# Seven sums of squares moved half a block or a whole block later in TensorE's order

## The chip, the cores and the metric

The program runs on one core of a Trainium2 chip. The metric is the device time of one execution in microseconds (us), and lower is better. PE is TensorE, DVE is VectorE, ACT is ScalarE, POOL is GpSimd, SP is the engine that issues the weight transfers.

## The reference

Two transformer blocks run one after the other on 256 tokens of width 1024. All projections are dense matrix products with a normed activation; there are five feed-forward layers (one with a convolution, four with SwiGLU), a recurrence with its own attention, a gated chunk mixer, and two cross-attentions onto a memory of 256 rows. What matters here is the norm in front of a projection:

```python
def rms_norm(x, g):
    x32 = x.astype(jnp.float32)
    y = x32 * lax.rsqrt(jnp.mean(x32 * x32, axis=-1, keepdims=True) + RMS_EPS)
    return (y * g.astype(jnp.float32)).astype(x.dtype)

def swiglu_ffn(h, w_in, w_out):
    gate, up = jnp.split(h @ w_in, 2, axis=-1)
    return (jax.nn.silu(gate) * up) @ w_out

# per layer
x = x + 0.5 * swiglu_ffn(rms_norm(x, ffn1_norm[i]), ffn1_w_in[i], ffn1_w_out[i])
...
x = x + memory_cross_attention_2(rms_norm(x, xattn_norm[i]), mem_k, mem_v, xattn_wq[i], xattn_wo[i])
x = x + 0.5 * swiglu_ffn(rms_norm(x, ffn2_norm[i]), ffn2_w_in[i], ffn2_w_out[i])
```

## The kernel before

**The stream of weights.** The activations lie feature by feature over the 128 partitions, 8 tiles of 256 tokens. All weights come as 288 blocks of 1 MB in one fixed order. SP loads a block into one of two buffers `raw` as soon as DVE has finished with the block two before. A block has two halves ("pieces") of 1024 columns. ACT copies a piece to `wh`, rounded to the matmul's format (function `high`, L1267), DVE takes the difference `raw - wh` into `wl` (function `low`, L1890), and PE multiplies with three products per tile pair (`split_mm`, L282): 24 matmuls of 128x256 for a piece, 48 for a block. There are four slots of `wh` and `wl`, so the copies of block b+2 (issued by `high(b)` and `low(b)`) wait until PE is done with the same half of block b (semaphore `piece_done`).

**Late norms.** Seven of the norms are "late": `ffn0`, `ffn1`, `x0`, `ffn2`, `ffn3`, `x1` and `ffn4` (five feed-forward layers and two cross-attentions, in this order in time: ffn0, ffn1, x0, ffn2, ffn3, x1, ffn4). There the product runs with the activation that has only its gain, and the factor `rstd` is multiplied into the result, so PE need not wait for it. Meanwhile ACT squares x in two halves, DVE sums each half over its 4 tiles (`norm_parts`, L1919, one reduction for each half, into `work`), and PE sums over the partitions with a matrix of ones (`norm_sum`, L371, one fp32 matmul for each half; the page counts each as two). ACT then makes `rstd` from the sum with a Ln (L1299) and an Exp (L1306), each behind an `ACT_TABLE_LOAD`.

**Orders around a late norm.** Each engine runs its own list in the order written. PE in a feed-forward layer: first block, `norm_sum`, second block, four small matmuls that clear the accumulators (L409, behind a wait for `norm_var`, which the Ln sets), then steps of two blocks of the up projection and one of the down projection. In `ffn1` the sum of another norm (`mem2`) and a third sum (`first_norm_sum`, 16 rows at L379) stand at the same place. PE in a cross-attention: query block 0, `norm_sum`, query blocks 1 and 2, scores of head 0 (L920, which wait until DVE has scaled query block 0 with `rstd`), query block 3, and so on. DVE stands in front of every such place with the `low` of the second block, then the reduction of the second half of the squares, then the `low` of the third block, then the wait for `rstd`. ACT: `late_norm`, `high` of the third block, Ln, Exp, then in a feed-forward layer `early` (a Silu or the convolution's middle tap), `high` of the fourth block, `late`; in a cross-attention the `high` of the fourth block and of the next segment's first.

Of the kernel before, what the change touches and what calls it, by code (L numbers as in the profile page):

```python
# [51 lines left out]
BANKS = 4  # L52
# [222 lines left out]
def tensor_program(pe, t, s):  # L275
# [46 lines left out]
                              start=hf == 0 and tb == 0 and kk == 0, stop=k == KT - 1, weights_move=True)  # L322
        mm.then_inc(s["piece_done"], 1)

    def up_block(n, bank, b, act, name=None):
        for hf in range(2):
            up_piece(n, bank, b, hf, act, name)

    def token_block(n, bank, b, act, name=None):
# [55 lines left out]
    def ffn(f, seg, name):  # L385
# [10 lines left out]
                mm.then_inc(s["piece_done"], 1)  # L396

        up_block(n, n % BANKS, b, norm_parts, name)
        if f == 1:
            norm_sum("mem2")  # L400
        norm_sum(name)
        if f == 1:
            first_norm_sum(name)
        up_block(n + 1, (n + 1) % BANKS, b + 1, norm_parts)
        pe.wait_ge(s["norm_var"], NORM[name] + 1)
        if f == 0:
            pe.wait_ge(s["zero_row"], 1)
# [201 lines left out]
    for hf in range(2):  # L609
        w = piece(b, hf)  # L610
        for kk in range(4):
            k = 4 * hf + kk
# [333 lines left out]

    def memory_attention(i, name):
        project(f"xq{i}", norm_parts, n=1, name=name)
        norm_sum(name)
        project(f"xq{i}", norm_parts, first=1, n=2)  # L950
        scores, turn, mix = memory_heads(i)
        scores(0)
        project(f"xq{i}", norm_parts, first=3, n=1)
        scores(1)
        scores(2)
        turn(0)
        scores(3)
        for h in range(1, XA_H):
            turn(h)
            mix(h - 1)  # L960
        mix(XA_H - 1)
        for k in range(4):
            n = SEG[f"xo{i}"] + k
            bank_free(n)
            for hf in range(2):
                w = piece(BLK[f"xo{i}"] + k, hf)
                for kk in range(4):
                    c = 4 * hf + kk
                    if k == 0 and c % 2 == 0:
                        pe.wait_ge(s["att_low"], NA_H + CA_H + XA_H * i + c // 2 + 1)  # L970
                    for j in range(2):
                        mm = split_mm(ps[:, n % BANKS, j * T:(j + 1) * T],
                                      [x[:, kk * 256 + j * P:kk * 256 + (j + 1) * P] for x in w],
                                      [t.page_r[q][:, c * T:(c + 1) * T] for q in (2, 1)],
                                      start=c == 0 and j == 0, stop=c == KT - 1)
                mm.then_inc(s["piece_done"], 1)
# [275 lines left out]
def scalar_program(act, a, t, s):  # L1252
# [17 lines left out]
    def highs(seg, first=0, n=4):  # L1270
        for k in range(n):
            high(BLK[seg] + first + k)
# [297 lines left out]
    def ffn(fi, seg, early, late, prev=None, end=lambda *step: None):  # L1570
# [7 lines left out]
        if fi == 1:  # L1578
            joint_root(seg)
        else:  # L1580
            norm_root(seg)
        early(0, 0, 0, True)
        high(b + 1)
        late(0, 0, 0, True)
        end(0, 0, 0, True)

# [240 lines left out]

    def memory_attention(i, prev=None):
        late_norm(f"x{i}", prev)
        highs(f"xq{i}", n=1)  # L1830
        norm_root(f"x{i}")
        highs(f"xq{i}", 1, 2)
        memory_heads(i)
        highs(f"xo{i}", n=3)

# [39 lines left out]
def vector_program(dve, t, s):  # L1875
# [715 lines left out]

    def memory_attention(i, then, prev=None):
        late_norm(f"x{i}", prev)
        lows(f"xq{i}", n=1)
        dve.wait_ge(s["norm_std"], NORM[f"x{i}"] + 1)

        def query(k):
            if k:
                low(BLK[f"xq{i}"] + k)
            dve.wait_ge(s["piece_done"], 2 * (BLK[f"xq{i}"] + k) + 2)  # L2600
            scaled(t.page[0][:, k * 512:(k + 1) * 512],
                   ps[:, (SEG[f"xq{i}"] + k) % BANKS, :].rearrange("p (n t) -> p n t", n=2),
                   2).then_inc(s["u_evac"], 1)

        for k in range(3):
            query(k)
        memory_heads(i, query)
        residual(f"xo{i}", then=then)
# [238 lines left out]
```

## Time and profile before

| | us |
|---|---|
| three runs | 2081.5, 2084.69, 2081.97 |
| median | 2081.97 |
| the profiled execution | 2084.6 |
| its span | 2082.5 |
| PE busy | 1941.3 (93%) |
| DVE busy | 1331.4 (64%) |
| ACT busy | 1054.2 (51%) |
| mean granted clock | 0.978 |

The span is the time between the first and the last instruction in the trace; 2.1 us of the execution lie around it. A timeline row gives the start, the duration, the engine, the line, the operation and its operands, a count, and in brackets how long the engine sat idle before it and who ended that. The three runs differ by 3.2 us.

### The profile page before, as it was taken

How to read it: one execution, taken by the hardware profiler on the slowest of the kernel's cores; microseconds unless marked ns; L12 is line 12 of the kernel's file. 1: busy time of each engine (PE TensorE's matmuls, PEld its weight loads, DVE VectorE, ACT ScalarE, POOL GpSimd, SP SyncE). 2: the span in 40 equal slices, each digit the busy share in tenths (PEclk: the TensorE clock that was granted, in tenths of full speed). 3: DMA queues.
4: the chain of work that ended last, by engine and by line, in shares of the span. 5: the costliest groups of instructions: out<-in, count | busy, mean ns of one | idle time of the engine just before them, and what ended most of it. 6: DMA issues, size and time to landing. Idle time of an engine off the chain costs nothing.

```text
span 2082.5 us, 43630 instructions
## 1 busy us (share of the span) xinstructions
PE 1941.3 (93%) x18364; PEld 1894.7 (91%) x18364; DVE 1331.4 (64%) x1652; ACT 1054.2 (51%) x1373; POOL 56.9 (3%) x44
## 2 busy tenths in 40 slices
PE   5989997799998999998989899999999798999998
PEld 5988997799998999988888899999999797999998
DVE  6486579577777755698454656557555646556555
ACT  6555565745555544567522645445444455445443
POOL 0020000000000000000051000000000000000000
PEclk9999999899999999999999999999999899999999
DMA  5743332154554455443400335554445353434453
GB/s 196 223 152 140 132 132 102 61 183 162 184 186 149 166 181 181 169 155 120 164 5 3 144 120 182 181 181 163 181 181 183 124 183 116 160 124 166 183 183 113
DMA packets 51880, 313.35 MB, mean 150 GB/s; under 512 B 13488, under 2 KB 13616, under 8 KB 14256
## 3 DMA queue, kind: packets, MB, share of 16 engines
q1 hardware_dynamic: 51328, 308.42, 41.6%
q10 hardware_dynamic: 432, 3.15, 0.4%
q8 instruction: 97, 1.59, 0.3%
q14 instruction: 23, 0.19, 0.0%
HBM read 310.50 MB, written 1.05 MB: 150 GB/s over the span
## 4 chain that ended last, share of the span: by engine, by line
PE 68%; DVE 19%; ACT 6%; issue 4%; DMA 2%; DVEq 0%; ACTq 0%; SPq 0%
PE ps L282 60%; DVE wl L1890 6%; ACT wh L1267 2%; DMA raw<-in_stream 2%; PE ps L766 2%; DVE pages L2327 1%; DVE work L1919 1%; DVE pages L2147 1%; DVE pages L2149 1%; PE ps L941 1%; DVE pages L1963 1%; DVE pages L2389 1%; DVE h L1928 1%; DVE pages L2183 1%; DVE h_r L1948 1%
## 5 line engine op out<-in xcount | busy, mean ns | idle before, releaser
L1890 DVE TENSOR_TENSOR wl<-raw,wh 128x1024 fp32r<-128x1024 f32 x576 | 700.0, 1231 | 540.1 <-ACT wh L1267 538.4
L1267 ACT ACTIVATE wh<-raw 128x1024 fp32r<-128x1024 f32 x576 | 597.2, 1052 | 466.2 <-PE ps L282 403.5
L282 PE MATMUL ps<-sq_r,wh 128*128 128x256 f32 x2592 | 743.1, 287 | 17.9 <-DVE h_r L1907 8.3
L282 PE MATMUL ps<-sq_r,wl 128*128 128x256 f32 x2592 | 735.9, 284 | 0.0
L282 PE MATMUL ps<-h_r,wh 128*128 128x256 f32 x2560 | 727.1, 284 | 0.0
L282 PE MATMUL ps<-pages_r,wh 128*128 128x256 f32 x2480 | 550.4, 288 | 39.3 <-DVE pages_r L1907 18.4
L282 PEld LDWEIGHTS ps<-sq_r,wh 128*128 128x128 f32 x2592 | 500.2, 193 | 22.9 <-issue 18.9
L282 PEld LDWEIGHTS ps<-sq_r,wl 128*128 128x128 f32 x2592 | 500.1, 193 | 0.0
L282 PEld LDWEIGHTS ps<-h_r,wh 128*128 128x128 f32 x2560 | 494.2, 193 | 0.5
L282 PE MATMUL ps<-pages_r,wl 128*128 128x256 f32 x1680 | 480.6, 286 | 0.0
L282 PEld LDWEIGHTS ps<-pages_r,wh 128*128 128x128 f32 x2480 | 427.8, 196 | 43.5 <-issue 32.2
L282 PEld LDWEIGHTS ps<-pages_r,wl 128*128 128x128 f32 x1680 | 327.9, 195 | 0.0
L282 PE MATMUL ps<-work_r,wh 128*128 128x256 f32 x976 | 272.3, 286 | 0.0
L282 PEld LDWEIGHTS ps<-work_r,wh 128*128 128x128 f32 x976 | 187.3, 195 | 0.1
L1568 ACT ACTIVATE pages_r<-work 128x512 fp32r<-128x512 f32 x55 | 34.7, 632 | 152.2 <-DVE work L2362 124.2
L1645 ACT ACTIVATE work<-work 128x512 f32<-128x512 f32 x44 | 27.8, 632 | 76.6 <-DVE work L1963 76.5
L282 PE MATMUL ps<-wh,sq_r 128*128 128x256 f32 x224 | 64.1, 286 | 0.0
L282 PE MATMUL ps<-wh,h_r 128*128 128x256 f32 x224 | 63.4, 283 | 0.0
L282 PE MATMUL ps<-wl,sq_r 128*128 128x256 f32 x224 | 63.4, 283 | 0.0
L2246 DVE TENSOR_TENSOR work_r<-work,pages_r 128x512 fp32r<-128x512 f32 x55 | 38.1, 693 | 38.4 <-ACT pages_r L1568 38.4
L1624 ACT ACTIVATE pages<-pages,param 128x256 f32<-128x256 f32 x44 | 24.1, 595 | 49.0 <-DVE pages L1963 49.0
L1279 ACT ACTIVATE pages_r<-pages 128x512 fp32r<-128x512 f32 x48 | 29.8, 630 | 37.0 <-DVE pages L2389 23.0
(309 smaller groups left out, 1814.3 us busy)
## 6 DMA issues: line engine op xcount, KB each, us to landing
raw<-in_stream SPq DMA_DIRECT2D x288, 1024.0 KB, 4.8
pages<-in_rpb SPq DMA_DIRECT2D x32, 64.0 KB, 6.7
pages<-in_mem SPq DMA_DIRECT2D x1, 1024.0 KB, 5.3
x<-in_x SPq DMA_DIRECT2D x1, 1024.0 KB, 12.8
pages<-in_mem ACTq DMA_DIRECT2D x1, 1024.0 KB, 4.9
pages<-in_gmlp_b ACTq DMA_DIRECT2D x1, 1024.0 KB, 4.5
pages<-in_gmlp_w ACTq DMA_DIRECT2D x1, 1024.0 KB, 6.7
out<-h SPq DMA_DIRECT2D x4, 256.0 KB, 2.4
```

The source lines that it names most:

```text
L282: mm = pe.matmul(out, left, right, start=start and q == 0, stop=stop and q == 2, skip_group_check=True)
L766: mm = pe.matmul(ps[rows[par], bank + e, turned * 256 + u * CH:turned * 256 + (u + 1) * CH], left, right, start=True, stop=True)
L941: mm = pe.matmul(ps[:, memory_bank(i, "out", h), c * T:(c + 1) * T], t.page[15][:, at_:at_ + P], memory_turned(t, h)[:, mb * T:(mb + 1) * ...
L1267: f(t.wh[(2 * b0 + hf) % PIECE_SLOTS][:], t.raw[b0 % 2][:, hf * 1024:(hf + 1) * 1024], ACT.Copy).then_inc(s["high_done"], 1)
L1279: f(dst[:, c], src[:, c], ACT.Copy).then_inc(s["op_high"], 1)
L1568: f(hidden_parts(t, k)[0], t.work[:, k * 512:(k + 1) * 512], ACT.Copy).then_inc(s["hidden_high"], 1)
L1624: ins = f(t.page[k][:, j * T:(j + 1) * T], t.page[13][:, k * 1024 + j * T:k * 1024 + (j + 1) * T], ACT.Identity, scale=w, bias=bias)
L1645: f(gate_, gate_, ACT.Silu).then_inc(s["gate_ready"], 1)
L1890: tt(t.wl[i][:], t.raw[b0 % 2][:, hf * 1024:(hf + 1) * 1024], t.wh[i][:].bitcast(F32), ALU.subtract).then_inc(s["low_done"], 1)
L1919: dve.tensor_reduce(norm_partial(t, name)[:, hf * T:(hf + 1) * T], squares[:, hf * 1024:(hf + 1) * 1024].rearrange("p (k t) -> p t k", k=4 ...
L1928: stt(dst[:, c], src[:, c], par(t, gain[0], gain[1] + k), t.rstd[:] if rstd is None else rstd, ALU.mult, ALU.mult).then_inc(s["norm_out"], 1)
L2246: tt(low_, t.work[:, k * 512:(k + 1) * 512], high_.bitcast(F32), ALU.subtract).then_inc(s["hidden_ready"], 1)
```

## The change

The sum of squares leaves its place behind the first block. In the five feed-forward layers it stands behind the first half of the second block, with the other sums of `ffn1`; `up_block` gets a callback for that. In the two cross-attentions it stands behind query block 1, a whole block later. On ACT the `high` of the fourth block goes ahead of `early` in the feed-forward layers, and ahead of Ln and Exp in the cross-attentions; DVE's `low` of that block goes ahead of the wait for `rstd` in the cross-attentions. No instruction is added or removed.

```diff
--- before.py
+++ after.py
@@ -322,8 +322,10 @@
                               start=hf == 0 and tb == 0 and kk == 0, stop=k == KT - 1, weights_move=True)
         mm.then_inc(s["piece_done"], 1)
 
-    def up_block(n, bank, b, act, name=None):
+    def up_block(n, bank, b, act, name=None, between=lambda: None):
         for hf in range(2):
+            if hf:
+                between()
             up_piece(n, bank, b, hf, act, name)
 
     def token_block(n, bank, b, act, name=None):
@@ -396,12 +398,15 @@
                 mm.then_inc(s["piece_done"], 1)
 
         up_block(n, n % BANKS, b, norm_parts, name)
-        if f == 1:
-            norm_sum("mem2")
-        norm_sum(name)
-        if f == 1:
-            first_norm_sum(name)
-        up_block(n + 1, (n + 1) % BANKS, b + 1, norm_parts)
+
+        def sums():
+            if f == 1:
+                norm_sum("mem2")
+            norm_sum(name)
+            if f == 1:
+                first_norm_sum(name)
+
+        up_block(n + 1, (n + 1) % BANKS, b + 1, norm_parts, between=sums)
         pe.wait_ge(s["norm_var"], NORM[name] + 1)
         if f == 0:
             pe.wait_ge(s["zero_row"], 1)
@@ -946,8 +951,9 @@
 
     def memory_attention(i, name):
         project(f"xq{i}", norm_parts, n=1, name=name)
+        project(f"xq{i}", norm_parts, first=1, n=1)
         norm_sum(name)
-        project(f"xq{i}", norm_parts, first=1, n=2)
+        project(f"xq{i}", norm_parts, first=2, n=1)
         scores, turn, mix = memory_heads(i)
         scores(0)
         project(f"xq{i}", norm_parts, first=3, n=1)
@@ -1579,8 +1585,8 @@
             joint_root(seg)
         else:
             norm_root(seg)
+        high(b + 1)
         early(0, 0, 0, True)
-        high(b + 1)
         late(0, 0, 0, True)
         end(0, 0, 0, True)
 
@@ -1827,9 +1833,9 @@
 
     def memory_attention(i, prev=None):
         late_norm(f"x{i}", prev)
-        highs(f"xq{i}", n=1)
+        highs(f"xq{i}", n=2)
         norm_root(f"x{i}")
-        highs(f"xq{i}", 1, 2)
+        highs(f"xq{i}", 2, 1)
         memory_heads(i)
         highs(f"xo{i}", n=3)
 
@@ -2591,11 +2597,11 @@
 
     def memory_attention(i, then, prev=None):
         late_norm(f"x{i}", prev)
-        lows(f"xq{i}", n=1)
+        lows(f"xq{i}", n=2)
         dve.wait_ge(s["norm_std"], NORM[f"x{i}"] + 1)
 
         def query(k):
-            if k:
+            if k > 1:
                 low(BLK[f"xq{i}"] + k)
             dve.wait_ge(s["piece_done"], 2 * (BLK[f"xq{i}"] + k) + 2)
             scaled(t.page[0][:, k * 512:(k + 1) * 512],
```

The first place is PE at the start of `ffn2`; `sq_r` and `h_r` are the two parts of the activation, `wh` and `wl` those of the weights, and `low_done` is set by DVE's difference. Before:

```order
L282 MATMUL ps<-sq_r_50,wh 128x256
L282 MATMUL ps<-h_r_49,wh 128x256
L282 MATMUL ps<-sq_r_50,wl 128x256
L371 MATMUL ps<-work,const 128x256 [waits norm_part] x2
L282 MATMUL ps<-sq_r_50,wh 128x256 [waits low_done,u_evac]
L282 MATMUL ps<-h_r_49,wh 128x256
L282 MATMUL ps<-sq_r_50,wl 128x256
```

And the same place of the changed kernel, where a block's start is the row that waits for `u_evac` too, and a second half's start waits for `low_done` alone:

```order
L282 MATMUL ps<-sq_r_50,wh 128x256
L282 MATMUL ps<-h_r_49,wh 128x256
L282 MATMUL ps<-sq_r_50,wl 128x256
L373 MATMUL ps<-work,const 128x256 [waits norm_part] x2
L282 MATMUL ps<-sq_r_50,wh 128x256 [waits low_done]
L282 MATMUL ps<-h_r_49,wh 128x256
L282 MATMUL ps<-sq_r_50,wl 128x256
```

The sum stood in front of the second block and stands now in front of that block's second half, 24 matmuls later.

The second place is ACT in the cross-attention `x0`. `wh2`, `wh3` are the slots of the third block at first; `wh0`, `wh1` then take the fourth. Before:

```order
L1267 ACTIVATE wh2<-raw1 128x1024 [waits piece_done,raw_in1]
L1267 ACTIVATE wh3<-raw1 128x1024 [waits piece_done]
L1299 ACT_TABLE_LOAD
L1299 ACTIVATE rstd<-ps,stat 128x256 [waits norm_sum]
L1306 ACT_TABLE_LOAD
L1306 ACTIVATE rstd<-rstd 128x256 [waits norm_var]
L1267 ACTIVATE wh0<-raw0 128x1024 [waits piece_done,raw_in0]
L1267 ACTIVATE wh1<-raw0 128x1024 [waits piece_done]
```

And now:

```order
L1273 ACTIVATE wh2<-raw1 128x1024 [waits piece_done,raw_in1]
L1273 ACTIVATE wh3<-raw1 128x1024 [waits piece_done]
L1273 ACTIVATE wh0<-raw0 128x1024 [waits piece_done,raw_in0]
L1273 ACTIVATE wh1<-raw0 128x1024 [waits piece_done]
L1305 ACT_TABLE_LOAD
L1305 ACTIVATE rstd<-ps,stat 128x256 [waits norm_sum]
L1312 ACT_TABLE_LOAD
L1312 ACTIVATE rstd<-rstd 128x256 [waits norm_var]
```

The two copies of query block 3 have moved ahead of the first table load, so Ln and Exp stand behind a wait for PE's query block 1.

## Rows read from the trace of the kernel before

**Rows 1.** The page: busy time, and the chain that ended last by engine

```profile
PE 1941.3 (93%) x18364; PEld 1894.7 (91%) x18364; DVE 1331.4 (64%) x1652; ACT 1054.2 (51%) x1373; POOL 56.9 (3%) x44
...
PE 68%; DVE 19%; ACT 6%; issue 4%; DMA 2%; DVEq 0%; ACTq 0%; SPq 0%
```

**Rows 2.** Waits of PE: line waited for: us in total, times, longest us

```profile
PE ps L371 <- DVE work L1919: 21.8, 11, 9.2
```

**Rows 3.** Timeline of PE where ffn2 starts: start, duration, instruction, [idle before]

```profile
1250.57 0.60 PE L371 MATMUL ps<-work,const 128*128 128x256 f32 x2
1252.44 0.70 PE L371 MATMUL ps<-work,const 128*128 128x256 f32 x2 [1.27 <-DVE work L1919]
1252.79 0.47 PE L282 MATMUL ps<-sq_r,wh 128*128 128x256 f32 x1
```

**Rows 4.** Timeline of PE at norm mix1, a sum that found its input ready

```profile
870.43 1.03 PE L371 MATMUL ps<-work,const 128*128 128x256 f32 x4
871.11 0.47 PE L282 MATMUL ps<-pages_r,wh 128*128 128x256 f32 x1
```

**Rows 5.** Timeline of PE at ffn0, ffn1, x0, ffn3, x1, ffn4

```profile
470.05 0.48 PE L371 MATMUL ps<-work,const 128*128 128x256 f32 x1 [1.27 <-DVE work L1919]
...
674.96 0.48 PE L371 MATMUL ps<-work,const 128*128 128x256 f32 x1 [0.85 <-DVE work L1919]
...
1186.93 0.48 PE L371 MATMUL ps<-work,const 128*128 128x256 f32 x1 [1.27 <-DVE work L1919]
...
1447.46 0.48 PE L371 MATMUL ps<-work,const 128*128 128x256 f32 x1 [1.69 <-DVE work L1919]
...
1820.05 0.48 PE L371 MATMUL ps<-work,const 128*128 128x256 f32 x1 [1.26 <-DVE work L1919]
...
1885.57 0.48 PE L371 MATMUL ps<-work,const 128*128 128x256 f32 x1 [1.29 <-DVE work L1919]
```

**Rows 6.** Stretches: PE, PEld, DVE, ACT, POOL busy (count), granted clock, DMA share, GB/s

```profile
688.00:860.00 172.00, 172.00 (x1436) 172.00 (x1435) 108.53 (x123) 76.11 (x85) 0.00 (x0) 1.00 0.51 183
1180.00:1200.00 20.00, 18.73 (x149) 18.16 (x148) 13.85 (x16) 13.11 (x15) 0.00 (x0) 1.00 0.44 165
1260.00:1438.00 178.00, 178.00 (x1486) 178.00 (x1485) 105.34 (x110) 76.89 (x86) 0.00 (x0) 1.00 0.51 180
```

**Rows 7.** Timeline of ACT, then PE, in ffn0

```profile
472.64 0.42 ACT L1306 ACTIVATE rstd<-rstd 128x256 f32<-128x256 f32 x1
...
476.52 1.06 ACT L1267 ACTIVATE wh<-raw 128x1024 fp32r<-128x1024 f32 x1 [0.67 <-PE ps L282]
...
477.02 0.47 PE L282 MATMUL ps<-sq_r,wh 128*128 128x256 f32 x1
...
506.95 0.39 PE L282 MATMUL ps<-pages_r,wh 128*128 128x256 f32 x1 [0.78 <-DVE wl L1890]
```

**Rows 8.** Timeline of ACT, DVE and PE in the cross-attention x0

```profile
1186.44 1.28 ACT L1299 ACT_TABLE_LOAD   x1
1187.73 0.47 ACT L1299 ACTIVATE rstd<-ps,stat 128x256 f32<-128x256 f32 x1
...
1189.52 0.42 ACT L1306 ACTIVATE rstd<-rstd 128x256 f32<-128x256 f32 x1
1190.60 1.06 ACT L1267 ACTIVATE wh<-raw 128x1024 fp32r<-128x1024 f32 x1 [0.66 <-PE ps L282]
...
1186.79 2.35 DVE L1890 TENSOR_TENSOR wl<-raw,wh 128x1024 fp32r<-128x1024 f32 x2
1189.97 0.69 DVE L1963 TENSOR_TENSOR pages<-ps,rstd 128x512 f32<-128x512 f32 x1 [0.82 <-ACT rstd L1306]
...
1198.98 0.38 PE L920 MATMUL ps<-pages 128*128 128x256 f32 x1
```

**Rows 9.** SP's issues at x0, and all issues of 1180 to 1200 us with landing

```profile
1185.19 4.45 SPq L240 DMA_DIRECT2D raw<-in_stream  x2
...
raw<-in_stream SPq DMA_DIRECT2D x3, 1024.0 KB, 4.9
```

## The prediction

> **What bounds the kernel now.** I read the page first. PE is busy 93% of the span and the chain that ended last is 68% PE, 19% DVE [rows 1]: time is won only where PE stands still, and what another engine does counts only where PE waits for it. So the second view is PE's waits. One of them is the waits of the sums of squares for DVE's reductions: 21.8 us in 11 waits, the longest 9.2 [rows 2]. That one and three more, 12.9 us, belong to norms that the change leaves alone, at the start of the program and at mix2. The other seven are the late norms, one idle time each: 1.27 in ffn2 [rows 3], and 1.27, 0.85, 1.27, 1.69, 1.26 and 1.29 in the other six [rows 5], together 8.90 us. In the timeline the pattern is always the same: PE ends a block, does the sum of the first half, waits for the reduction of the second half, and goes on.
>
> **What one wait is worth.** The idle time in brackets counts from the modelled end of a matmul, so I measure from start to start. In ffn2 the sum starts at 1250.57 and the next block at 1252.79, 2.22 us [rows 3]. At mix1, where both halves are ready, the same four matmuls take 870.43 to 871.11, 0.68 us [rows 4]. The difference is 1.54 us, which is the bracket's 1.27 plus 0.27. I take bracket plus 0.27 at all seven places: 8.90 + 7 x 0.27 = 10.79 us. The gap alone, 8.90, is the lower end if the 0.27 is an artefact of how ends are modelled.
>
> **Is the input ready at the new place?** A matmul of the stream takes 172.00 / 1436 = 0.12 us [rows 6], so half a block is 2.88 us and a block 5.76. The old waits ended 1252.44 - 1250.57 = 1.87 us after the first block [rows 3]; in ffn3 with its longer bracket 0.42 later, 2.29. Both lie before 2.88, so the sum finds its input ready in the feed-forward layers, by 0.6 us at worst, and in the cross-attentions by 3.9. In ffn1 the reduction has even more time, since the sum of mem2 still goes first.
>
> **Are the weights of the second block ready earlier?** PE now starts the second block some 2.2 us sooner. DVE's list has the `low` of that block ahead of the reduction for which PE waited, so those weights were complete while PE still stood in the old wait. At x0 the transfer that follows this `low` is issued at 1185.19 [rows 9], which dates the `low` at about 1185.1; the first block ended at 1186.93 - 1.87 = 1185.06 [rows 5]. The first half's difference is one instruction of 2.35 / 2 = 1.18 us [rows 8] earlier, so PE has it, and needs the second half only 2.88 us later. I cost this at nothing.
>
> **What comes later: the factor rstd.** Ln and Exp hang on the sum. In ffn0 the second pair of the sum starts at 470.05 [rows 5] and the Exp ends at 472.64 + 0.42 = 473.06 [rows 7], 3.01 us behind. The same distance stands at x0: 1186.93 and 1189.94 [rows 5, 8]. In ffn0 the pair now starts at 468.18 (470.05 - 1.87) + 2.88 + 0.34 = 471.40, and rstd comes at 474.41, 1.35 us later than before though PE is 1.54 ahead. Who needs it?
>
> - In ffn1 to ffn4 PE needs nothing from rstd until the first down projection, two blocks (11.5 us) after the clearing matmuls. The Silu is now behind two weight copies and comes some 3 us later, but DVE's own list had the `low` of the same block between the gate's scale and the product, so the product stays where it was or comes earlier. That all these loops run without a gap shows the cover: PE is busy 172.00 of 172.00 and 178.00 of 178.00 us behind the starts of ffn1 and ffn2 [rows 6]. I cost it at nothing.
> - In ffn0 ACT and DVE are behind. There PE waits at 506.95, with a bracket of 0.78, for a weight difference [rows 7]. The stream of blocks would have brought it there at 505.82 (it starts the third block at 477.02 [rows 7], and five blocks of 48 matmuls by 0.12 are 28.8), so it loses 1.13 us. Back from there ACT and DVE hand over to each other without a wait for PE as far as the ACT copy at 476.52, which did wait for PE [rows 7]. That copy is the second of the fourth block. Now it can start when the Exp and the first copy are done, 474.41 + 0.9 = 475.3, and DVE takes it up 1.1 us earlier than before. So that chain gains 1.1 and not 1.54; the wait at 506.95 grows by 0.4.
>
> **The cross-attentions.** Here the margin is small. In x0 the first block ends at 1185.06. Query block 1 ends at 1190.82; the sum is in before ACT needs it. ACT copies the second half of query block 3 when PE has finished block 1. Before, such a copy began 0.44 us behind PE's last issue (the second pair of the sum at 1186.93 and 0.35 for it as in rows 3 give 1187.28, with 2.88 for half a block 1190.16; the copy is at 1190.60 [rows 8]), so now at 1191.26, and takes 1.06: 1192.32. Then come load, Ln, load and Exp, 1186.44 to 1189.94 in the old trace, 3.50 us [rows 8]: 1195.82. DVE's scale of 0.69 [rows 8] ends at 1196.54. PE asks for it at 1190.82 + 0.68 + 5.76 = 1197.26 (before: 1198.98 [rows 8], with 8 us to spare). The margin is 0.7 us; x1 has the same durations and so the same margin. The transfer of query block 3 is issued at 1185.19 and lands after 4.9 [rows 9], at 1190.1, ahead of 1191.26. Everything behind the scores is tied to PE's end of query block 3, through a copy, a difference and a softmax, and so moves with PE. I cost it at nothing; if the margin is missed by 1 us each time, it costs 2.
>
> One rule speaks against that margin. In the trace the load takes 1.28 us and the Ln starts at 1187.73, 0.01 us behind its end [rows 8]. The Trainium skill (ScalarE: Activation LUTs, What ACT_TABLE_LOAD costs) adds a drain of about 1.38 us to the same 1.28 for every switch to a different set. By the page the path to the scores would be 2.8 us longer, 2 us too late in each cross-attention. The trace has no such pause at any of these loads, and the old path was measured whole, so the sum goes by the rows.
>
> **The sum.** 10.79 less 0.4 in ffn0 is 10.4 us; I take 10.3. The profiled execution would go from 2084.6 (span 2082.5) to 2074.3. It lies 2.6 us above the median of its three companions; the gain is a sum of waits, not a share, so it is taken off the median as it is: 2081.97 - 10.3 = 2071.7 us. Bounds: upwards the full 10.8; downwards the bare gaps with the same loss in ffn0, 8.90 - 0.4 = 8.5, and another 1.3 if cutting the second block in two costs a new change of operands each time, at half of the 0.35 that a pair of the sum and the way back into the stream take together (1252.44 to 1252.79 [rows 3], seven times 0.18). That gives 7.2. The likeliest case's own range is 2071.2 to 2074.8.
>
> **Rivals.**
>
> 1. *The scores come to wait for rstd.* The 0.7 us margin is the difference of some eight terms. If ACT reaches the Ln 2 us later than I work out, PE loses 1.3 us at each of two places, and if in ffn0 the chain keeps its old place, another 1.1: 10.3 - 2.6 - 1.1 = 6.6 saved, 2075.4. For it: the third block's copies and the transfer come close to the fourth's. Against: all terms are durations of the same instructions at the same place.
> 2. *The gain is given back.* PE arrives earlier everywhere, and the later Silu makes the first down projection of ffn2, ffn3 and ffn4 wait, as ffn0's chain does now. Then their 1.54 + 1.96 + 1.56 = 5.1 go, and ffn0's 1.1: 4.1 saved, 2077.9. Against: the flat 178.00 of 178.00 [rows 6], and the 11.5 us until that projection.
> 3. *The drain of 1.38 us shows only where the Ln does not wait for the sum.* In the old x0 the first load was over at 1187.72, when the sum was just coming in, so a pause there could hide, though one behind the second load could not. The first pause is bared now: 1.38 more against a margin of 0.7 costs 0.7 at x0 and x1, 8.9 saved, 2073.1. It falls inside the own range, so it changes the chance and not the range.
> 4. *Slower: PE's clock.* The granted clock is 1.00 in the stretch around x0 although PE is busy 18.73 of 20.00 us there [rows 6], and the mean over the span is 0.978, so elsewhere it does drop. If the denser stream brought a drop from 2.4 to 1.2 GHz over one such stretch of 20 us in the middle of x0, those 18.7 us of PE work would take as long again, 18.7 more, and the whole would be 18.7 - 10.3 = 8.4 slower, 2090.4. It decides from 10.3 us of PE work at the lower level on. Against: the longest unbroken stretches, which are denser than anything the change makes, hold 1.00 [rows 6].
>
> That the change does nothing would need the waits to move along with the sum. The input comes 2.29 us after the first block at the latest (ffn3), ahead of the new place in every case, so they can't.
>
> **Chances.** Forecast 0.74 (rival 3 within it, 0.04), rival 1 0.13, rival 2 0.09, rival 4 0.04. A measurement of this kernel tells a difference of about 0.2% (4.2 us) from none: 2077.8 is the border. The forecast and rival 1 are below it, rival 2 lies on it and counts as no change, the slower rival lies above. Faster 0.87, same 0.09, slower 0.04. For the range I add the spread of a median (the three runs differ by 3.2 us) to the own range and reach over rival 1: 2069.3 to 2076.5.
>
> **What would show it.** Right: in each of the seven places the sum follows a run of 24 or 48 matmuls of the second block without a bracket, and block, sum and rest of the block take 0.68 us beyond 0.12 a matmul. PE's waits lose 8.9 us at this line and keep 12.9. The wait near 506 moves to about 505.8 and its bracket grows to about 1.2. The scores of head 0 in x0 and x1 show no bracket. Wrong: a bracket at the scores with ACT's Exp or DVE's scale behind it (rival 1 or 3), one at the first down projection with DVE's hidden part (rival 2), a granted clock under 1.00 between 450 and 700, 1180 and 1260, or 1440 and 1460 us (rival 4).

## The result, and the profile after

| | before | after |
|---|---|---|
| median of 7 and 7 runs | 2081.50 us | 2071.43 us |
| lowest to highest | 2080.85 to 2085.82 | 2068.48 to 2076.19 |
| the profiled execution (span) | 2084.6 (2082.5) | 2075.23 (2073.2) |

The ratio is 0.9949, with a 95% interval of 0.9937 to 0.9962. The change saves 10.1 us; the forecast was 2071.7. In the two further sets of runs that are told below the changed kernel took 2069.35 against 2081.51, and 2071.86 against 2080.93. The mean of the three differences is 10.4 us.

The page of the changed kernel, busy time and the chain that ended last (it answers to [rows 1]):

```profile
PE 1942.1 (94%) x18364; PEld 1898.6 (92%) x18364; DVE 1331.4 (64%) x1652; ACT 1054.5 (51%) x1373; POOL 57.0 (3%) x44
...
PE 73%; DVE 16%; ACT 5%; issue 4%; DMA 1%; DVEq 0%; ACTq 0%; SPq 0%
```

The counts are those of before and the busy times nearly so; the chain has changed: 5 points have gone from DVE, ACT and DMA to PE. The waits of PE for the reductions, which the four unchanged norms keep (it answers to [rows 2]; the line has moved from L371 to L373):

```profile
PE ps L373 <- DVE work L1925: 13.2, 4, 8.9
```

21.8 us in 11 waits have become 13.2 in 4. Now PE where ffn2 starts, in the changed kernel (it answers to [rows 3]); the third row is the clearing matmuls, which end the second block, the last one the stream behind them:

```profile
1251.30 1.03 PE L373 MATMUL ps<-work,const 128*128 128x256 f32 x4
1251.97 0.47 PE L282 MATMUL ps<-sq_r,wh 128*128 128x256 f32 x1
...
1255.04 1.04 PE L414 MATMUL ps<-zrow 128*128 128x512 bf16 x4
1255.73 0.47 PE L282 MATMUL ps<-sq_r,wh 128*128 128x256 f32 x1
```

And the same clearing matmuls in the kernel before:

```profile
1258.73 1.04 PE L409 MATMUL ps<-zrow 128*128 128x512 bf16 x4
```

This is the comparison on which the result rests: not how long a bracket is, but how long PE takes from the end of the first block to the same instruction behind the second. I call it the place's total. Before, it is 1258.73 - 1250.57 [rows 3] = 8.16 us. After, the first block ends 2.88 us (half a block) ahead of the sum, at 1248.42, and the total is 1255.04 - 1248.42 = 6.62. (PE's rows between are 0.12 us apart without a break at all seven places, so a half block does take 2.88 and, in the cross-attentions, the whole one 5.76.) The sum itself takes 1251.97 - 1251.30 = 0.67, as at mix1 [rows 4]; another 0.19 is lost at the second stream matmul behind it, which starts 0.31 us after the first and not 0.12. That stands behind the old place too, so it cancels in the gain. In the other six places the four matmuls also stand in one row, without a bracket (they answer to [rows 5]):

```profile
471.21 1.03 PE L373 MATMUL ps<-work,const 128*128 128x256 f32 x4
...
674.64 1.03 PE L373 MATMUL ps<-work,const 128*128 128x256 f32 x4
...
1190.20 1.03 PE L373 MATMUL ps<-work,const 128*128 128x256 f32 x4
...
1444.36 1.03 PE L373 MATMUL ps<-work,const 128*128 128x256 f32 x4
...
1817.78 1.03 PE L373 MATMUL ps<-work,const 128*128 128x256 f32 x4
...
1878.87 1.03 PE L373 MATMUL ps<-work,const 128*128 128x256 f32 x4
```

| place | total before | total after | gain | forecast (bracket + 0.27) |
|---|---|---|---|---|
| ffn0 | 8.16 | 6.62 | 1.54 | 1.54 |
| ffn1 | 12.05 | 10.94 | 1.11 | 1.12 |
| x0 (to the scores) | 13.92 | 12.38 | 1.54 | 1.54 |
| ffn2 | 8.16 | 6.62 | 1.54 | 1.54 |
| ffn3 | 8.58 | 6.62 | 1.96 | 1.96 |
| x1 (to the scores) | 13.90 | 12.38 | 1.52 | 1.53 |
| ffn4 | 8.18 | 6.62 | 1.56 | 1.56 |
| sum | | | 10.77 | 10.79 |

In ffn0 part of it is given back at the late wait (PE and DVE in the changed kernel; it answers to the last row of [rows 7]):

```profile
474.95 1.04 PE L414 MATMUL ps<-zrow 128*128 128x512 bf16 x4
...
505.93 0.39 PE L282 MATMUL ps<-pages_r,wh 128*128 128x256 f32 x1 [1.14 <-DVE wl L1896]
...
500.77 3.97 DVE L1925 TENSOR_REDUCE pages<-pages 128x256 f32<-128x1024 f32 x2 [0.26 <-ACT pages L1301]
504.67 2.34 DVE L1896 TENSOR_TENSOR wl<-raw,wh 128x1024 fp32r<-128x1024 f32 x2
```

The bracket has grown from 0.78 to 1.14. From the clearing matmuls to this wait's end it is now 505.93 - 474.95 = 30.98 us, against 30.62 before (476.33, the clearing matmuls' start there, to 506.95 [rows 7]), so 0.36 is given back. What is left of ffn0's gain, 1.18, also arrives at the end of the layer: from the end of its first block to the end of PE's next long wait it was 658.10 - 468.17 = 189.93 us and is 657.10 - 468.33 = 188.77. 10.77 - 0.36 = 10.4 us is what the seven places and the late wait are worth together.

The margin in x0, in ACT, DVE and PE of the changed kernel (it answers to [rows 8]):

```profile
1189.36 2.10 ACT L1273 ACTIVATE wh<-raw 128x1024 fp32r<-128x1024 f32 x2 [3.54 <-DMA raw<-in_stream]
1191.48 1.28 ACT L1305 ACT_TABLE_LOAD   x1
1192.78 0.47 ACT L1305 ACTIVATE rstd<-ps,stat 128x256 f32<-128x256 f32 x1
1193.27 1.28 ACT L1312 ACT_TABLE_LOAD   x1
1194.56 0.42 ACT L1312 ACTIVATE rstd<-rstd 128x256 f32<-128x256 f32 x1
...
1195.01 1.29 DVE L1969 TENSOR_TENSOR pages<-ps,rstd 128x512 f32<-128x512 f32 x2 [2.20 <-ACT rstd L1312]
...
1196.82 1.46 PE L925 MATMUL ps<-pages 128*128 128x256 f32 x6
```

The first of DVE's two scalings ends at about 1195.01 + 0.65 = 1195.66, and PE starts the scores at 1196.82 without a bracket, so about 1.1 us are left, where the forecast had 0.7. The same rows decide the rival from the Trainium skill (ScalarE: Activation LUTs, What ACT_TABLE_LOAD costs). The first load starts 0.02 us behind the end of the copy ahead of it (1191.46) and ends at 1192.76; the sum had been complete since about 1191.2, and the Ln starts at 1192.78. Here nothing but the load could hide a pause, and there is none on either side of it: the load costs its 1.28 us, and the drain of about 1.38 us, which the Trainium skill adds to it at the same place, does not show. The page and the measurement differ, and in this kernel the measurement decides. (The page states the drain for a switch to a different set; that each of these loads is one, the trace does not show.)

### The profile page after: what moved, and what is told of

The parts are those of the page before. It is cut to its first block, busy times and chain, and to the rows that moved or that the text cites. A ratio compares the mean times of both kernels' runs of the same rounds, so it can differ in the third digit from the quotient of the medians.

```text
span 2073.2 us, 43630 instructions
## 1 busy us (share of the span) xinstructions
PE 1942.1 (94%) x18364; PEld 1898.6 (92%) x18364; DVE 1331.4 (64%) x1652; ACT 1054.5 (51%) x1373; POOL 57.0 (3%) x44
## 4 chain that ended last, share of the span: by engine, by line
PE 73%; DVE 16%; ACT 5%; issue 4%; DMA 1%; DVEq 0%; ACTq 0%; SPq 0%
PE ps L282 64%; DVE wl L1896 4%; ACT wh L1273 2%; PE ps L771 2%; DVE pages L2333 2%; DMA raw<-in_stream 1%; DVE pages L2153 1%; DVE pages L2395 1%; DVE pages L2155 1%; DVE pages L1969 1%; DVE pages_r L1913 1%; PE ps L946 1%; PE ps L757 1%; DVE pages L2189 1%; PE ps L469 1%
```

## The experiments

Each was timed in turn with the kernel before on the same chip; a difference "to the changed kernel" is one to its median of 2071.43, which comes from another set of runs.

### The sum's place alone

The changed kernel, with the edits of ACT's and DVE's lists taken back:

```diff
-        high(b + 1)
         early(0, 0, 0, True)
+        high(b + 1)
...
-        highs(f"xq{i}", n=2)
+        highs(f"xq{i}", n=1)
         norm_root(f"x{i}")
-        highs(f"xq{i}", 2, 1)
+        highs(f"xq{i}", 1, 2)
...
-        lows(f"xq{i}", n=2)
+        lows(f"xq{i}", n=1)
...
-            if k > 1:
+            if k:
```

> The kernel before with the sums moved in PE's order alone; ACT and DVE keep their old order. My theory (the gain is the wait for DVE's reduction, the copies matter only in ffn0's chain): ffn1, ffn2, ffn3, ffn4, x0 and x1 show no bracket at the sum and save 1.1, 1.54, 1.96, 1.55, 1.54, 1.54 us as in the changed kernel. In x0 the Exp then comes at the sum's second pair + 3.0 us, about 1.6 us earlier than in the changed kernel. In ffn0 the factor comes 1.35 us later than before and the two copies of the fourth block still stand behind the convolution's tap, so DVE's chain is about 0.7 us later than before instead of 1.1 earlier: the bracket near 506 us grows from 0.78 to about 3.0 and ffn0 loses 0.7. Total about 8.5 us under before, 1.8 over the changed kernel. Rival (the copies ahead of the gate are what wins): little gain, under 3 us.

Measured: 2072.56 us (5 runs, 2070.15 to 2075.04), ratio 0.9955 (0.9942 to 0.9968). All seven places have the totals of the changed kernel, to 0.02 us. The difference is in ffn0, in PE's rows:

```profile
474.37 1.04 PE L414 MATMUL ps<-zrow 128*128 128x512 bf16 x4
...
507.10 0.39 PE L282 MATMUL ps<-pages_r,wh 128*128 128x256 f32 x1 [2.39 <-DVE wl L1896]
```

32.73 us from one to the other, 1.75 more than in the changed kernel, and 1.72 of it are still there at the end of PE's next long wait (190.49 us behind the first block, against 188.77); the expectation had 1.8 of time, and a longer bracket than the 2.39 that showed. So PE's order brings the gain at the seven places, and the weight copies ahead of the convolution's first gate are worth 1.75 us, by keeping ACT's and DVE's chain in ffn0 from falling back. In the cross-attentions the copies are worth nothing by themselves: x0's total is 12.38 with and without.

### The copies alone

The kernel before, with ACT's and DVE's lists as in the changed kernel, and PE's order untouched (the diff above, with its signs turned, on the kernel before).

> The kernel before with the copies moved in ACT's and DVE's order alone; the sums stay behind the first block. My theory: every bracket at the sums stays (1.27, 0.85, 1.27, 1.27, 1.69, 1.26, 1.29), the second copy of the fourth block waits for PE as before, and the total is within 1 us of before; in x0 and x1 the factor comes so late (Ln behind a copy that waits for PE's query block 1, Exp's end about 1198.0 where it was 1189.9) that the scores at 1198.98 are just met or wait up to 0.3 us. Rival (the copies win part of it): 2 to 5 us faster.

Measured: 2083.38 us (11 runs, 2080.75 to 2086.23), ratio 1.0008 (0.9999 to 1.0016). PE's waits in it:

```profile
PE ps L371 <- DVE work L1919: 21.8, 11, 9.1
```

The 1.9 us by which its median lies above that of before are more than the 1 us expected, but the interval holds 1 and no place shows them (the profiled execution took 2080.8). No wait has gone, and none has come: the late one in ffn0 keeps its bracket of 0.78, and x0's total is 13.92 as before. The two parts are not additive: the copies save nothing alone and 1.75 us once PE is ahead.

### A quarter instead of a half

The changed kernel, with the sum behind the first quarter of the second block, in the cross-attentions too (behind a quarter of query block 1):

```diff
+            if kk == 2 and hf == 0:
+                quarter()
             operand_part(name, k)
...
         for hf in range(2):
-            if hf:
-                between()
-            up_piece(n, bank, b, hf, act, name)
+            up_piece(n, bank, b, hf, act, name, quarter=between)
...
-        project(f"xq{i}", norm_parts, first=1, n=1)
-        norm_sum(name)
+        at1 = SEG[f"xq{i}"] + 1
+        up_block(at1, at1 % BANKS, BLK[f"xq{i}"] + 1, norm_parts, between=lambda: norm_sum(name))
```

> The changed kernel with the sum behind the first quarter of the second block (12 matmuls, 1.44 us) at all seven places. My theory: the reduction is ready 1.87 us after the first block (2.29 in ffn3, and in ffn1 later in terms of its own pair), so a wait of about 0.4 us from start to start is left at ffn0, x0, ffn2, x1, ffn4, 0.85 at ffn3 and about 0 in ffn1: a bracket of about 0.15 (the bracket is 0.27 less), 0.6 at ffn3. Together 2.9 us of the gain is lost in PE's waits; ffn0's factor comes 1.0 us earlier than in the changed kernel, so its chain may win some back. Total 7.5 to 8.5 us under before. Rival (the gain comes from elsewhere than the wait, for instance from the cover of the weights): as the changed kernel, 10 us.

Measured: 2073.91 us (5 runs, 2070.40 to 2075.46), ratio 0.9959 (0.9946 to 0.9972). One bracket is left, in ffn3; the rows of ffn2 and of ffn3 in this kernel:

```profile
1246.03 1.21 PE L373 MATMUL ps<-work,const 128*128 128x256 f32 x4
...
1251.39 1.04 PE L414 MATMUL ps<-zrow 128*128 128x512 bf16 x4
...
1439.27 0.60 PE L373 MATMUL ps<-work,const 128*128 128x256 f32 x2
1440.20 0.70 PE L373 MATMUL ps<-work,const 128*128 128x256 f32 x2 [0.34 <-DVE work L1925]
```

In ffn3 the pairs start 0.93 us apart and not 0.34: 0.59 lost. In ffn2 the first block ends at 1246.03 - 1.44 = 1244.59 and the total is 6.80, 0.18 above the half's, with no bracket; the row of the sum, 1.21 long and not 1.03, has it. The same 0.2 shows in ffn0, ffn4, x0 and x1, and nothing in ffn1. My expectation was too high by more than a factor of two: it let the input meet the sum's start at 1.44 us, and forgot that the second pair, the only one that is late, stands 0.34 behind the first. With it PE asks at 1.78; the inputs come at 1.87 and, in ffn3, 2.29, which makes 0.1 and 0.5. Against that the sum is earlier, and ffn0's late wait keeps the old 30.62 us and 0.78. By these rows the loss is near 1.1 us to the changed kernel. The medians of the same set are 4.6 us apart (2069.35 for the changed kernel); with five and six runs that reach from 2066.82 to 2076.01 they can't tell 1.1, and no place shows the rest. So the arrival times of [rows 3, 5] are right: a quarter is just too early, a half is late enough by 0.6 us in ffn3 and by 1.0 in the other places.

### The whole block

The changed kernel, with the feed-forward layers' sum behind the whole second block:

```diff
         for hf in range(2):
-            if hf:
-                between()
             up_piece(n, bank, b, hf, act, name)
+        between()
```

> The changed kernel, but in the feed-forward stages the sum stands behind the whole second block, right ahead of the clear; the two memory-attention stages keep the sum behind half of query block 1. If the time gained is only that of a sum that is late enough for the square sums, this is as good as the changed kernel (0 us). My theory says that a later sum has a price of its own, since the clear and all that follows needs the variance made from it: after the sum's last matmul about 0.8 to 1.0 us pass until the variance is there, so PE shows a wait of 0.8 to 1.0 us at the clear in ffn1, ffn2, ffn3 and ffn4 (3.6 us in all), and in ffn0 the chain from the sum through ScalarE and VectorE to the late wait near 505 us runs 2.9 us later, which that wait shows in full (from 1.1 to about 4 us). Together about +6.4 us over the changed kernel: 2071.4 + 6.4 = 2077.8 us, 3.7 us under the kernel before. No wait at any sum.

Measured: 2078.65 us (9 runs, 2075.82 to 2086.31), ratio 0.9984 (0.9968 to 1.0000). Its waits of PE at the clearing matmuls:

```profile
PE ps L413 <- ACT rstd L1304: 3.2, 4, 0.8
PE ps L413 <- DVE pages L2258: 0.8, 1, 0.8
```

And its timeline of PE (with its weight loads, PEld) in ffn2, and of PE in ffn0:

```profile
1255.94 1.03 PE L372 MATMUL ps<-work,const 128*128 128x256 f32 x4
1257.53 0.55 PEld L413 LDWEIGHTS ps<-zrow 128*128 128x128 bf16 x4 [0.97 <-ACT rstd L1304]
1257.76 0.82 PE L413 MATMUL ps<-zrow 128*128 128x512 bf16 x3 [0.80 <-ACT rstd L1304]
1258.23 0.47 PE L282 MATMUL ps<-sq_r,wh 128*128 128x256 f32 x1
...
506.43 0.39 PE L282 MATMUL ps<-pages_r,wh 128*128 128x256 f32 x1 [2.41 <-DVE wl L1895]
...
657.96 0.58 PE L282 MATMUL ps<-pages_r,wh 128*128 128x256 f32 x1 [5.79 <-DVE work_r L2251]
```

The wait stands at all five clears, not four as I had written. (In the cross-attentions the sum stays where the changed kernel has it, behind the whole of query block 1, not behind half of it as the expectation says.) The bracket of 0.80 is too long: there are four weight loads but only three matmuls, so the record of the first clearing matmul is missing in this trace, and the row starts with the second. So I compare the stream matmul behind the clear: 1258.23 - 1250.18 (the end of the first block, 5.76 us ahead of the sum) = 8.05 us, against 1255.73 - 1248.42 = 7.31 in the changed kernel. That is 0.74 more, and the same to 0.01 us at the other clears: 2.97 us in ffn1 to ffn4. In ffn0 the late wait ends 40.40 us behind the first block (466.03), against 37.60, so that chain is 2.8 later, as expected (2.9). Behind this wait something came that I had not costed, PE's clock (columns as in [rows 6], the third number from the right is the granted clock):

```profile
507.30:510.40 3.10, 3.10 (x16) 3.10 (x16) 0.93 (x3) 2.19 (x4) 0.00 (x0) 0.50 0.43 140
```

In these 3.1 us the clock is at the lower of its two levels (1.2 GHz and not 2.4), and the stream's matmuls start 0.21 us apart and not 0.12: 16 times 0.09, or about 1.5 us. The kernel with the sum's place alone had a bracket of 2.39 at the same instruction and 1.00 behind it, so the drop does not come each time. Part is given back in the next long wait, which has shrunk from 6.66 to 5.79: to its end ffn0 takes 657.96 - 466.03 = 191.93 us against 188.77, 3.16 more. Together 6.1 (forecast 6.4); the medians differ by 7.2. So the new place is not good for being late: the gain of 10.4 falls to about 4 when the sum moves by another 2.88 us. Between "too early" (1.44) and "too late" (5.76) the half is the only boundary of a piece; three quarters, inside a piece, were not tried.

### The cross-attentions' sum later

The changed kernel, with the sum behind query block 2:

```diff
-        project(f"xq{i}", norm_parts, first=1, n=1)
+        project(f"xq{i}", norm_parts, first=1, n=2)
         norm_sum(name)
-        project(f"xq{i}", norm_parts, first=2, n=1)
```

> The changed kernel, but in the two memory-attention stages the sum stands behind the whole of query block 2 instead of behind query block 1 (1.5 blocks' worth later than needed); the feed-forward stages keep the change. This takes the margin of the first rival: the scores of head 0 wait for the scaled queries, which wait for the rstd that comes from the sum. In the changed kernel the first scaled queries are ready about 1.1 us before PE asks for the scores. The sum's second pair now ends about 5.8 us later in PE's order than before, so Exp and the scaling end later by as much less the copy work that ScalarE now has behind it, and PE should wait about 3.4 us ahead of the first scores in x0 and in x1: 2 x 3.4 = 6.8 us over the changed kernel, 2071.4 + 6.8 = 2078.2 us. If the scores hung on something else (the copies, the memory's keys), the place total would stay at 12.4 us and the time at 2071.4 us.

Measured: 2078.34 us (8 runs, 2074.57 to 2084.14), ratio 0.9981 (0.9964 to 0.9997). PE in x0, and the row of x1's scores:

```profile
1195.67 1.03 PE L373 MATMUL ps<-work,const 128*128 128x256 f32 x4
1199.72 1.65 PE L925 MATMUL ps<-pages 128*128 128x256 f32 x3 [3.02 <-DVE pages L1968]
...
1202.90 0.47 PE L282 MATMUL ps<-sq_r,wh 128*128 128x256 f32 x1
...
1830.54 0.89 PE L925 MATMUL ps<-pages 128*128 128x256 f32 x2 [3.02 <-DVE pages L1968]
```

Two blocks (11.52 us) ahead of 1195.67 the first one ends, at 1184.15; the total is 15.57 against 12.38, 3.19 us lost in each of the two: 6.4 (forecast 6.8), and the medians differ by 6.9. But the wait is not all that the place costs in this trace. Behind it the clock is at its lower level:

```profile
1199.70:1202.90 3.20, 3.18 (x8) 2.56 (x9) 3.20 (x4) 1.13 (x2) 0.00 (x0) 0.51 0.00 0
```

The eight matmuls of the scores and the way back take 1202.90 - 1199.72 = 3.18 us, and 1198.36 - 1196.82 = 1.54 in the changed kernel, whose clock is 1.00 there. In x1 it is much the same (a clock of 0.57 from 1830.50 to 1833.40). From the end of its first block to that of the next layer's, x0 takes 68.80 us against 63.98 and x1 68.94 against 63.97: 9.8 us and not 6.4. This execution took 2083.21 us, 4.9 above the median of its eight; whether the faster ones kept their clock, no trace shows, so the closeness of 6.9 to 6.4 proves little. That each wait costs 3.19 is shown by its rows. The first rival's mechanism is real, the scores do hang on `rstd` through ACT and DVE. Only its condition was not met in the change, by 1.1 us.

### mem2's squares in ffn0

Two tries to win the 1.14 us of ffn0's late wait. In the changed kernel DVE does two reductions of `mem2`, 3.97 us, right ahead of the copy that PE waits for (500.77 in the rows of the result). The first try moves them and their squares behind the next step, the second moves half of them; ACT's list has the same edits:

```diff
-                if fi == 0 and k == 0:
-                    norm_parts("mem2", t.page[8])
+                if fi == 0 and k == 1:                      # first try
+                    norm_parts("mem2", t.page[8])
...
+                if fi == 0:                                 # second try
+                    norm_parts("mem2", t.page[8], (k,))
```

> The changed kernel with one more edit: in ffn0 the squares and partial sums of mem2 stand one step later in the order of ScalarE and VectorE, behind the next chunk of the ffn's own work. In the changed kernel PE's late wait in ffn0 (1.14 us near 505.9 us) is for a low part that VectorE writes, and the chain to it is loaded by mem2's squares. If that work sits in the chain, the wait goes (0 to 0.2 us) and the time falls by about 1.1 us to 2070.3 us. If the chain is set by something else, the wait stays at 1.1 us. Should the later sums of mem2 be needed sooner than I think, a new wait appears behind 520 us.

Measured: 2070.49 us (5 runs, 2065.46 to 2072.34), ratio 0.9938 (0.9925 to 0.9952). PE's waits in ffn0:

```profile
519.55 0.39 PE L282 MATMUL ps<-pages_r,wh 128*128 128x256 f32 x1 [0.27 <-DVE wl L1896]
...
532.01 0.39 PE L282 MATMUL ps<-sq_r,wh 128*128 128x256 f32 x1 [0.68 <-DVE wl L1896]
...
654.34 0.58 PE L282 MATMUL ps<-pages_r,wh 128*128 128x256 f32 x1 [6.87 <-DVE work_r L2252]
```

The wait at 505.9 is gone, and two new ones take its place, 0.95 together. That is the warning at the end of the expectation, not its sum.

> The changed kernel with mem2's squares and partial sums in ffn0 split: the first half of them at the end of one step, the second half at the end of the next (the run before this one moved both together by a step, and moved the wait with them, from 1.14 us near 505.9 us to 0.27 and 0.68 us near 519.6 and 532.0 us). VectorE's share is two reductions of together 3.97 us ahead of copies for which PE waits 1.14 us; so PE's order has about 2.9 us of cover there. A half costs 2.0 us, under the cover, in each of the two steps. If cover is per step and is made up again between them, all waits for weight copies in ffn0 between 490 and 540 us are gone and the stretch from ffn0's clear to the end of ffn0's weights is 1.1 us shorter than in the changed kernel: 2071.4 - 1.1 = 2070.3 us. If VectorE's lag adds up over the two steps, PE waits at the second one for about what it waits now, and the gain is under 0.3 us. Either is too small to be told by the medians alone; the trace tells it.

Measured: 2071.89 us (6 runs, 2070.61 to 2075.77), ratio 0.9948 (0.9931 to 0.9966). PE's waits in ffn0:

```profile
522.73 0.39 PE L282 MATMUL ps<-pages_r,wh 128*128 128x256 f32 x1 [0.29 <-DVE wl L1896]
...
535.17 0.39 PE L282 MATMUL ps<-sq_r,wh 128*128 128x256 f32 x1 [0.68 <-DVE wl L1896]
...
657.47 0.58 PE L282 MATMUL ps<-pages_r,wh 128*128 128x256 f32 x1 [6.84 <-DVE work_r L2252]
```

And the last of these waits in the changed kernel:

```profile
657.10 0.58 PE L282 MATMUL ps<-pages_r,wh 128*128 128x256 f32 x1 [6.66 <-DVE work_r L2252]
```

The same two waits, at the same distance behind the sum (51.15 us from 471.58; in the first try 51.13 from 468.42). From the sum to the end of the next 1200 matmuls it is 179.05 us in both and 179.23 in the changed kernel: 0.18 us won there, so the second reading of the expectation holds, DVE's lag adds up over the steps. Even the 0.18 does not last: PE then waits for another result of DVE (`work_r`), 6.87 and 6.84 us and not 6.66, and that wait ends 185.92, 185.89 and 185.89 us behind the sum in the three kernels. Where in those two steps the 4 us of reductions stand does not matter, since DVE and ACT hand over to each other through both without room. Neither is a better kernel by any number that can be measured; moving the reductions out of ffn0 altogether was not tried.

### The changed kernel twice more

> The changed kernel once more, unchanged. The places won 10.4 us by the first pair of traces, the spans differ by 9.3. Theory: the rest is the granted clock behind PE's long waits (at 650 to 666, 1150 to 1160 and 1625 to 1645 us), which falls otherwise in every execution. Then this trace has the same intervals at the seven places within 0.05 us, and differs from the first by up to 1 us at each of those stretches. Rival: the change costs about 1 us at a place that I overlooked; then the same 1 us is missing at the same place again.

> The changed kernel once more, unedited, next to the run with mem2's halves on the same chip, as its base and as a third profiled execution. The seven places should each take what they took in the two traces of it before (6.62 us in ffn0, ffn2, ffn3 and ffn4, 10.93 us in ffn1, 12.38 us in x0 and x1) whatever the span is; the median should be 2069.4 to 2071.5 us, while the span may differ by up to 7 us from the first one of 2073.2 us, through stretches in which the granted clock is below 1 behind the long waits of PE near 130, 330 to 400, 640 and 980 us. If instead the places themselves vary, the spans' difference should be found in them.

Measured: 2069.35 us (6 runs, 2066.82 to 2076.01), ratio 0.9947 (0.9932 to 0.9962), span 2066.2; and 2071.86 us (6 runs, 2069.95 to 2073.93), ratio 0.9949 (0.9931 to 0.9968), span 2068.0. Three executions of one program have spans of 2073.2, 2066.2 and 2068.0 us. The places don't vary: x1 takes 12.38 in all three, and in ffn2 the stream goes on behind the clear 4.43 us after the sum's start in all three. (In the third trace the record of the first clearing matmul is missing, so the row of the clear itself stands 0.22 us late.) What varies lies between. From mix1's sum to x0's it is 1190.20 - 867.54 = 322.66 us in the first execution and 1186.57 - 867.91 = 318.66 in the third. The ends of PE's waits cut this stretch into parts that can be compared:

| from (first, third) | to | first | third | granted clock in the first 10 us, first and third |
|---|---|---|---|---|
| 867.54, 867.91 | 915.52, 915.88 | 47.98 | 47.97 | |
| 915.52, 915.88 | 940.57, 939.45 | 25.05 | 23.57 | 0.83 and 1.00 |
| 940.57, 939.45 | 981.31, 980.19 | 40.74 | 40.74 | |
| 981.31, 980.19 | 1017.25, 1014.76 | 35.94 | 34.57 | 0.84 and 1.00 |
| 1017.25, 1014.76 | 1153.29, 1150.50 | 136.04 | 135.74 | |
| 1153.29, 1150.50 | 1190.20, 1186.57 | 36.91 | 36.07 | 0.74 and 0.84 |

The stretch behind 915.52 in the first execution, and the same in the third (columns as in [rows 6]):

```profile
915.50:925.50 10.00, 9.97 (x71) 10.00 (x72) 10.00 (x16) 5.24 (x8) 0.00 (x0) 0.83 0.54 211
```

```profile
915.90:925.90 10.00, 10.00 (x83) 10.00 (x84) 9.97 (x17) 6.26 (x9) 0.00 (x0) 1.00 0.56 211
```

And the wait near 981, in the first and in the third:

```profile
981.31 0.55 PE L282 MATMUL ps<-wh,pages_r 128*128 128x256 f32 x1 [2.79 <-DVE wl L1896]
```

```profile
980.19 0.36 PE L282 MATMUL ps<-wh,pages_r 128*128 128x256 f32 x1 [1.36 <-DVE wl L1896]
```

Three parts in which the clock is lower make 1.48 + 1.37 + 0.84 = 3.7 of the 4.0 us, each of them behind the end of a wait of PE; the other 0.3 stand between 1017 and 1153. The wait near 981 is 1.43 us longer in the first execution and costs nothing: its part takes 40.74 us in both. PE only came to it earlier there, because its clock ahead of it was higher (0.72 against 0.50 from 970 to 976 us). All this is around long waits of PE that the change doesn't touch; the drop behind 915 is in neither expectation's list.

## Why the prediction was right

- **Which waits go.** Seven of eleven, and PE's waits at this line fell by 8.6 us (21.8 to 13.2) with the forecast's 8.9 less 0.3 of run-to-run change in the four that stay. The sum at its new place costs 0.67 (forecast 0.68). One sign was drawn too tight: block, sum and rest of the block should take 0.68 beyond 0.12 a matmul, and take 6.62 - 5.76 = 0.86. The forecast left out the 0.19 at the second stream matmul behind the sum; it is there before and after, so the gain is not touched.
- **What a wait is worth.** Bracket plus 0.27 was tried at seven places against start-to-start totals: 10.77 measured, 10.79 forecast. The lower bound, in which the 0.27 is an artefact of modelled ends, is out, and so is its price for cutting the second block in two.
- **When the input is ready.** 1.87 and 2.29 us after the first block: the quarter shows it from the other side.
- **ffn0.** Forecast: 0.4 given back, end of the wait at 505.8, bracket 1.2. Measured: 0.36, 505.93, 1.14. The copy that PE's progress allows earlier is the reason; without the reordered copies it would have been 0.36 + 1.75 = 2.1.
- **The cross-attentions.** No bracket at the scores; the margin was 1.1 and not 0.7. ACT's second copy ended about 7.0 us behind the first block and not 7.3, and PE asked for the scores at 12.38 and not 12.20 (the same 0.19). Rival 1 fell by its condition and not by its mechanism, which cost 3.2 us a place once the sum stood a block later, and 4.9 with the drop of the clock behind it.
- **Feed-forward layers 1 to 4.** Costed at nothing, and no new wait came; rival 2 falls. The room isn't large, though: a sum 2.88 us later costs 0.74 at each clear.
- **The drain behind a table load** (rival 3) does not show in these rows, neither where the load hides behind the sum nor where it is bared.
- **The clock** (rival 4): 0.978 as the mean before and 0.977 after, and 1.00 in both from 1180 to 1260 and from 1440 to 1460 us. The third stretch that the prediction named for it, 450 to 700, was badly chosen: it has 0.99 after, but also before, from a drop behind PE's wait near 657. The rival also had the cause the wrong way round. No denser stretch lowered the clock; what the runs show is the lower level behind waits, 0.51 behind one of 3.02 us and 0.50 behind one of 2.41, though not behind one of 2.39 in another execution.
- **The profiled executions** differ by 2082.5 - 2073.2 = 9.3 us, less than the 10.4 of the places. The 1.1 us between is inside what the stretches between the places do from one execution to the next (7 us in three spans of the same kernel), and so needs no term of the change.
- **What was luck.** The forecast of 2071.7 lies 0.3 us from the median of 2071.43. The medians of three sets of the same kernel are 2071.43, 2069.35 and 2071.86, so a hit that close is chance; what the rows bear out is the 10.4 of the places against the forecast's 10.3.

## What to carry to other kernels

A wait at the head of an in-order engine can be filled with work that is already there: measure when the input comes behind the last instruction ahead of the wait, and put the consumer behind just that much of the following stream, at the next boundary. Both edges cost, so look at the far one too: who hangs on the result, and how late it may become before that one is the wait. A reordering on the other engines may be worth nothing alone and something once the first engine is ahead, so try the parts both singly and together.

## What the runs showed that I had not expected

- A second pair of matmuls that came 0.09 us too early, by the arrival times, lost 0.18 us and showed no bracket (the quarter, ffn2). Short waits can be missing among the brackets; start-to-start distances have them.
- Moving 4 us of DVE work by a whole step, or by half of it, moved PE's wait to places 16 and 29 us further on, won 0.18 us there and nothing by the end of the layer. The bracket at an instruction tells where a lag becomes visible, not where it comes from.
- The span of one program varies by 7 us between executions at unchanged places. In the stretch that was taken apart it is PE's granted clock behind waits (0.83 against 1.00 in the same 10 us); a wait that is longer in one of them can cost nothing, since PE only came to it earlier.
- A wait can cost more than its length: behind 3.02 us of standing still PE's next 3.2 us ran at a clock of 0.51, and the place lost 4.9 us and not 3.2.
